# Four joins of a layer's output to x: last unit, root and first tiles by halves of the tokens

## The reference

```python
x = x + rms_norm(y, attn_post_g[layer])      # y = attention's output @ w_o
h = rms_norm(x, ffn_pre_g[layer])
f = swiglu(h, w_gate, w_up, w_down)
x = x + rms_norm(f, ffn_post_g[layer])       # then kv = rms_norm(x, kv_src_g) @ w_kv, or the next block
```

## Time and profile before

| | us |
|---|---|
| median of 3 runs | 1927.88 |
| the profiled execution | 1928.37 |
| its span | 1926.1 |
| TensorE busy, share of the span | 1908.9, 99% |
| VectorE | 954.8, 50% |
| ScalarE | 724.7, 38% |
| GpSimd | 738.0, 38% |

### The profile page before, as it was taken

The page is one execution under the profiler, slowest core; times in us unless marked ns, Lnnn a source line. Parts: engine busy times, 40 slices in busy tenths (PEclk is TensorE's granted clock), DMA queues, the critical chain, the costliest instruction groups (busy, mean ns, idle before and its releaser), DMA issues.

```text
span 1926.1 us, 22691 instructions
## 1 busy us (share of the span) xinstructions
PE 1908.9 (99%) x9056; PEld 1547.2 (80%) x9056; DVE 954.8 (50%) x1671; ACT 724.7 (38%) x1180; POOL 738.0 (38%) x313
## 2 busy tenths in 40 slices
PE   9999999999999999999999999999999999999998
PEld 7777888888888777888888888887777888888887
DVE  6662554442016545274444004796766755555203
ACT  6554422222234455342222224335654343333221
POOL 2333244444452322424444443343312444444442
PEclk9999999999999999999999999999999999999999
DMA  4512132223231222312222332321111223222232
GB/s 162 176 60 84 55 99 95 93 98 98 99 126 61 93 94 77 110 55 99 95 93 97 99 105 93 120 99 66 44 45 62 94 97 99 93 95 97 98 99 88
DMA packets 53305, 178.61 MB, mean 93 GB/s; under 512 B 5808, under 2 KB 8000, under 8 KB 52944
## 3 DMA queue, kind: packets, MB, share of 16 engines
q1 hardware_dynamic: 46928, 165.14, 26.1%
q10 hardware_dynamic: 6272, 12.02, 1.9%
HBM read 175.00 MB, written 6.33 MB: 94 GB/s over the span
## 4 chain that ended last, share of the span: by engine, by line
PE 96%; DVE 2%; ACT 1%; issue 1%; DMA 0%; SPq 0%; POOL 0%; DVEq 0%; ACTq 0%
PE bank L413 26%; PE bank L415 26%; PE bank L414 26%; PE bank L1563 2%; PE bank L1594 2%; PE bank L1548 1%; PE bank L1169 1%; PE bank L1163 1%; PE bank L1164 1%; PE bank L2024 1%; PE bank L1526 1%; PE bank L857 1%; PE bank L912 1%; PE bank L1046 1%; PE bank L1598 1%; PE bank L1040 1%
## 5 line engine op out<-in xcount | busy, mean ns | idle before, releaser
L393 POOL TENSOR_TENSOR wlo<-raw,whi 128x1024 fp32r<-128x1024 f32 x284 | 682.8, 2405 | 1140.1 <-ACT whi L388 1140.1
L388 ACT ACTIVATE whi<-raw 128x1024 fp32r<-128x1024 f32 x286 | 302.8, 1059 | 844.2 <-PE bank L415 813.0
L413 PE MATMUL bank<-hh,whi 128*128 128x512 f32 x1344 | 527.1, 392 | 1.2 <-DVE tmp L526 1.2
L415 PE MATMUL bank<-hh,wlo 128*128 128x512 f32 x1344 | 523.3, 389 | 0.0
L414 PE MATMUL bank<-hl,whi 128*128 128x512 f32 x1344 | 523.2, 389 | 0.0
L413 PEld LDWEIGHTS bank<-hh,whi 128*128 128x128 f32 x1344 | 252.3, 188 | 63.1 <-issue 9.8
L415 PEld LDWEIGHTS bank<-hh,wlo 128*128 128x128 f32 x1344 | 252.3, 188 | 52.6
L414 PEld LDWEIGHTS bank<-hl,whi 128*128 128x128 f32 x1344 | 252.4, 188 | 52.0 <-issue 0.5
L526 DVE TENSOR_TENSOR tmp<-bank,rs 128x512 f32<-128x512 f32 x154 | 105.3, 689 | 237.4 <-PE bank L415 223.5
L413 PE MATMUL bank<-fh,whi 128*128 128x512 f32 (+1 forms) x504 | 194.5, 386 | 0.0
L415 PE MATMUL bank<-fh,wlo 128*128 128x512 f32 (+1 forms) x504 | 194.5, 386 | 0.0
(11 more groups left out here) (304 smaller groups left out, 2475.3 us busy)
## 6 DMA issues: line engine op xcount, KB each, us to landing
raw<-stream SPq DMA_DIRECT2D x307, 512.0 KB, 3.4
bias_scratch<-rel_scratch ACTq DMA_DIRECT2D x1, 4096.0 KB, 18.1
biasB<-bias_scratch ACTq DMA_DIRECT2D x16, 256.0 KB, 2.8
w<-w_in ACTq DMA_DIRECT2D x2, 1024.0 KB, 5.8
x<-x_in SPq DMA_DIRECT2D x3, 512.0 KB, 9.3
out<-y SPq DMA_DIRECT2D x8, 128.0 KB, 1.9
out<-y ACTq DMA_DIRECT2D x8, 128.0 KB, 2.1
x<-x_in SPq DMA_DIRECT2D x2, 256.0 KB, 5.9
```

The source lines that it names most:

```text
L388: e.activation(slot[u][0][:, :], raw[u % 2][:, :], ACT.Copy).then_inc(*w_hi.done(u))
L393: e.tensor_tensor(slot[u][1][:, :], raw[u % 2][:, :], slot[u][0][:, :].bitcast(F32), ALU.subtract)\
L413: e.matmul(o, wh, h, start=first, stop=False)
L415: return e.matmul(o, wl, h, start=False, stop=last)
```

## The change

- The last unit of each of the four outputs is done by halves of the tokens: at oA and oB the last tile (`last_out_blocks_pe`), behind the down projections the last unit's four tiles (`last_down_pe`).
- Squares, sums, root, reciprocal and spread are made for each half by itself. Half 0's are interleaved with the products of half 1, and half 1's with the next layer's first products.
- The first tiles of the join (`AHEAD`: 2 at j0 and j2, 3 at j1 and j3) are done by halves, half 0 of all of them before half 1.
- `fill_clock` is no longer called at these four places.
- The copies of half 1 of the last four down tiles to y go from VectorE to ScalarE (`down_copy_act`).
- In the down projection's tail one unit is rounded, behind the root of half 0; the other is rounded in the join, behind the square of tile 1 (now in all four joins).
- Banks of the roots and of j1's and j3's squares are others.

```diff
-    def token_root_pe(e, key, spare, sums, ahead):
-        fill_clock(e, ahead, spare)
...
+    AHEAD = {"j0": 2, "j1": 3, "j2": 2, "j3": 3}
+    def root_sums_pe(e, key, half):
+        bk = bank[ROOT_AT[key][half]]
...
+        for t in tiles_of(half):
+            e.matmul(bk[:, t * P:(t + 1) * P], tmp[7][:, t * P:(t + 1) * P], ones, start=t == 2 * half, stop=False, skip_group_check=True)
+        e.wait_ge(*squared.at((key, KD - 1, half)))
+        for t in tiles_of(half):
+            mm = e.matmul(bk[:, t * P:(t + 1) * P], tmp[0][:, t * P:(t + 1) * P], ones, start=False, stop=t == 2 * half + 1, skip_group_check=True)
+        mm.then_inc(*summed.done((key, "tokens", half)))
...
     def out_pe(e, key, begun, ahead):
...
+        last_out_blocks_pe(e, u, 0, range(KD)).then_inc(*proj.done((key, KD - 1, 0)))
+        root_sums_pe(e, key, 0)
+        last_out_blocks_pe(e, u, 1, range(3))
+        root_spread_pe(e, key, 0)
+        last_out_blocks_pe(e, u, 1, range(3, KD)).then_inc(*proj.done((key, KD - 1, 1), ("unit", u)))
...
     def join_pe(e, key, outs, before):
...
+        half_high(0, 0)
+        root_sums_pe(e, before, 1)
+        half_low(0, 0)
+        half_high(1, 0)
+        e.wait_ge(*formed.at((key, "scaled", n - 1, 0)))
+        root_spread_pe(e, before, 1)
+        half_low(1, 0)
+        if n == 3:
+            half_high(2, 0)
+            half_low(2, 0)
+        half_high(0, 1)
+        for k in range(1, n):
+            half_high(k, 1)
+            half_low(k - 1, 1)
+        half_low(n - 1, 1)
+        for k in range(n, KD):
...
+    def join_act(e, key, before, gain, through, both=True):
+        n = AHEAD[key]
+        join_high_act(e, key, gain, 0, 0)
+        if before in ("oA", "oB"):
+            last_square_act(e, before, 1)
+        else:
+            down_last_act(e, before)
+        join_high_act(e, key, gain, 1, 0)
+        root_half_act(e, before, 1)
+        for k in range(2, n):
+            join_high_act(e, key, gain, k, 0)
+        for k in range(n):
+            join_high_act(e, key, gain, k, 1)
         for k in range(KD):
...
             square_tile(e, key, k, x[:, k, :], through)
-            if k == 1 and key in ("j0", "j2"):
+            if k == 1:
                 round_unit(e)
...
     def join_dve(e, key, before, post, gain, through, between=None):
+        e.wait_ge(*summed.at((before, "inverse", 0)))
+        join_half_tile(e, key, before, post, 0, 0)
+        if before not in ("oA", "oB"):
+            down_add_dve(e, before, 5, 1)
+            down_add_dve(e, before, 6, 1)
+        join_half_tile(e, key, before, post, 1, 0)
+        join_half_low(e, key, gain, 0, 0)
+        if before in ("oA", "oB"):
+            last_out_dve(e, before, 1)
+        join_half_low(e, key, gain, 1, 0)
+        root_half_dve(e, before, 1)
+        for k in range(2, n):
+            join_half_tile(e, key, before, post, k, 0)
+            join_half_low(e, key, gain, k, 0)
+        e.wait_ge(*summed.at((before, "inverse", 1)))
+        join_half_tile(e, key, before, post, 0, 1)
+        for k in range(1, n):
+            join_half_tile(e, key, before, post, k, 1)
+            join_half_low(e, key, gain, k - 1, 1)
+        join_half_low(e, key, gain, n - 1, 1)
+        for k in range(1, n - 1):
+            add_square(e, key, k, through)
+        join_tile(e, key, before, post, n)
...
+    def last_down_pe(e, key, u):
+        d = (key, "down")
+        for half, c in enumerate(HALVES):
+            for m in range(4, KD):
...
+                if half and m == 4:
+                    root_sums_pe(e, d, 0)
+                if half and m == 5:
+                    root_spread_pe(e, d, 0)
...
+    def down_tail_act(e, d):
+        e.wait_ge(*formed.at((d, "sq", 3)))
+        for m in range(4, KD):
+            down_square_act(e, d, m, 0)
+        down_square_act(e, d, 4, 1)
+        down_copy_act(e, d, 4)
+        root_half_act(e, d, 0)
+        round_unit(e)
+        for m in (5, 6):
+            down_square_act(e, d, m, 1)
+            if m == 5:
+                down_copy_act(e, d, m)
+
+    def down_last_act(e, d):
+        down_square_act(e, d, KD - 1, 1)
+        down_copy_act(e, d, 6)
+        down_copy_act(e, d, KD - 1)
```

More of the change, by code:

```diff
@@ new lines, in root_spread_pe, with root_half_act @@
+    def root_spread_pe(e, key, half):
+        e.wait_ge(*stats.at((key, "tokens", half)))
+        for t in tiles_of(half):
+            mm = e.matmul(bank[ROOT_AT[key][0]][:, t * P:(t + 1) * P], stat[:, 12 + t:13 + t].to_broadcast([P, P]), ident,
+                          start=True, stop=True)
+        mm.then_inc(*summed.done((key, "inverse", half)))
+    def root_half_act(e, key, half):
+        c = slice(2 * half, 2 * half + 2)
+        e.wait_ge(*summed.at((key, "tokens", half)))
+        e.activation(stat[:, 12 + 2 * half:14 + 2 * half], wide_sums(ROOT_AT[key][half])[:, c], ACT.Sqrt, scale=1.0 / D, bias=cc("eps"))\
+            .then_inc(*made.done((key, "root", half)))
@@ L1096, in token_root_dve, with last_out_blocks_pe @@
-    def token_root_dve(e, key):
-        e.wait_ge(*made.at((key, "root")))
-        e.reciprocal(stat[:, 12:16], stat[:, 12:16]).then_inc(*stats.done((key, "tokens")))
+    HALVES = (slice(0, T // 2), slice(T // 2, T))
+    LAST_BANK = (4, 5)
+    def last_out_blocks_pe(e, u, half, ks):
+        c = HALVES[half]
+        for k in ks:
+            mm = product(e, u, k, bank[LAST_BANK[half]][:, c], oh[:, k, c], ol[:, k, c], k == 0, k == KD - 1)
+        return mm
     def out_pe(e, key, begun, ahead):
@@ L1155, in of_high @@
             bk, out_key = outs[i]
             wh, wl = (w[:, k * P:(k + 1) * P] for w in slot[us[i]])
[L1157 to L1163, removed]
@@ L1222, in join_root_act, with join_tile @@
             round_unit(e)
[L1224 to L1233, removed]
+    def join_tile(e, key, before, post, k):
+        tb, r = 2 + k % 4, bank[ROOT_AT[before][0]]
+        e.tensor_tensor(tmp[tb][:, :], y[:, k, :], r[:, :], ALU.mult).then_inc(*formed.done((key, "scaled", k)))
         e.wait_ge(*formed.at((key, "scaled", k)))
@@ L1236, in join_tile, with join_half_tile @@
             .then_inc(*joined.done((key, k)))
-    def join_dve(e, key, before, post, gain, through, between=None):
-        e.wait_ge(*summed.at((before, "inverse")))
-        join_tile(e, key, post, 0)
-        for k in range(KD):
+    def join_half_tile(e, key, before, post, k, half):
+        tb, r, c = 2 + k % 4, bank[ROOT_AT[before][0]], HALVES[half]
+        e.tensor_tensor(tmp[tb][:, c], y[:, k, c], r[:, c], ALU.mult).then_inc(*formed.done((key, "scaled", k, half)))
+        e.wait_ge(*formed.at((key, "scaled", k, half)))
+        e.scalar_tensor_tensor(x[:, k, c], tmp[tb][:, c], gg(post, k), x[:, k, c], ALU.mult, ALU.add)\
+            .then_inc(*(joined.done((key, "half", k, 1), (key, k)) if half else joined.done((key, "half", k, 0))))
@@ L1283, in ffn_pe @@
                 end = kk == KF // 2 - 1 - (LAST_UNITS if conv and half else 0)
+                if end and half and not conv:
+                    last_down_pe(e, key, u)
+                    return
                 for r, m in ([(r, m) for m in range(4) for r in range(2)] if end
@@ L1601, in b_first_pe, with half_high, half_low @@
     def b_first_pe(e):
-        for k in range(KD):
-            if k % 2 == 0:
-                u = next_unit(e)
+        n, before = AHEAD["j1"], ("F0", "down")
+        us = [next_unit(e) for _ in range(2)]
+        def half_high(k, half):
+            e.wait_ge(*high.at(("j1", "half", k, half)))
+            for t in tiles_of(half):
+                if k == 0:
+                    join_free_pe(e, before, V_BANK[0][t])
+                values_high_pe(e, us[k // 2], 0, k, t)
+        def half_low(k, half):
+            e.wait_ge(*low.at(("j1", "half", k, half)))
+            for t in tiles_of(half):
+                mm = values_low_pe(e, us[k // 2], 0, k, t)
+            if k == 1 and half:
+                mm.then_inc(*proj.done(("unit", us[0])))
+        half_high(0, 0)
+        root_sums_pe(e, before, 1)
+        half_low(0, 0)
+        half_high(1, 0)
+        e.wait_ge(*formed.at(("j1", "scaled", n - 1, 0)))
+        root_spread_pe(e, before, 1)
+        half_low(1, 0)
+        half_high(2, 0)
+        half_low(2, 0)
+        half_high(0, 1)
+        for k in range(1, n):
+            half_high(k, 1)
+            half_low(k - 1, 1)
+        half_low(n - 1, 1)
+        for k in range(n, KD):
+            if k // 2 == len(us):
+                us.append(next_unit(e))
+            u = us[k // 2]
+            e.wait_ge(*high.at(("j1", k)))
             for t in range(QT):
-                if k:
-                    e.wait_ge(*high.at(("j1", k)))
-                else:
-                    e.wait_ge(*high.at(("j1", "half", t // 2)))
                 values_high_pe(e, u, 0, k, t)
```

243 lines of the change are left out of this document (143 added, 100 removed).

## The result

The changed kernel takes 1938.1 us (median of four runs, 1936.7 to 1940.5) against 1927.9: ratio 1.0054, 95% interval 1.0036 to 1.0071. It is 10.2 us slower; the forecast was 6.5 slower, 1934.4, with a range that ends at 1938.0. The sign and the waits came out as forecast. The size did not: there is one more cost on top of the waits, the clock, which the prediction had left out of its sum.

What follows compares the result with a forecast made beforehand. TensorE bounds the kernel, busy 1908.9 of 1926.1 us. Removed work of −12.6 us and added idle of +19.1 give +6.5 us, so 1934.4 against the median 1927.88; range 1925.5 to 1938.0.

Steps and rivals of the forecast that it cites:

- the waits: TensorE's idle at the four ends, walked through three in-order queues: 21.5 us against 2.4 before, +19.1.
- the clock: Rival (c), behind idle stretches at j1 and j3: 1.2 GHz for one tile each, +5.4, 1939.8 us; chance 0.10.
- The walk: Step-by-step timing of each of the four ends with prices read from the profile, counted from the last unit's first matmul.
- the walk's 12.10 and 16.76: Check on the kernel before: walked times of the join's first matmul (trace 12.28) and tile 3's late x (trace 16.85).
- The stops: VectorE's x and hl, with SBUF inputs, stand still while GpSimd's low part runs; six large ones of 1.71 to 1.86 us.
- Rival (a): GpSimd's part and x pass each other: 1925.6 us with no stop, 1928.6 or 1931.4 with one; chance 0.22.
- The bound that the prediction drew from the Trainium skill: Whichever of GpSimd and VectorE starts first keeps the shared ports, so a stop is at most a low part's 2.4 us.
- Work alone (rival b): At the four ends waits stay at 2.4 us and only the 12.6 us of removed work counts: 1915.3 us; chance 0.06.
- a clock under 1.00 beside the waits: Sign in the profile after that would show the forecast wrong: granted clock below 1.00 beside TensorE's waits near the joins.
- the argument "against": Against a falling clock: mean 0.89 after TensorE's last matmul, so the clock holds over a good part of an idle stretch.
- Fillers as waste: 66 of TensorE's 75 matmuls that compute nothing stand at the four ends and were counted as removable work.
- The 14.7 us: TensorE work gone at the four ends: 66 fillers at 0.2225 us each, −14.7 us, net −12.6 after added halves.

Runs made afterwards that it cites:

- three_fill: three_all with 69 matmuls that compute nothing in its gaps (14 before tile 3 at all joins, 9 and 4 before the first hh at j1 and j3): 1934.0 us.
- apart_both: The changed kernel with the down tail's rounding moved forward, the join's rounding moved back and square 1's add behind tile 3's low part: 1926.5 us, ratio 0.9992.
- low_split: The changed kernel with GpSimd's low part of the four units rounded at j1 and j3 cut into four quarter-width operations: 1931.5 us.
- three_all: The changed kernel with three tiles by halves at all four joins and the second half's reciprocal behind x of tile 2: 1944.2 us, two executions 1938.1 and 1938.6.
- no_fill: The kernel before the change without its 66 matmuls that compute nothing at the four ends: 1929.2 us, ratio 1.0006.
- best: apart_both with three tiles by halves at all joins, adds of squares 1 and 2 behind tile 3's hl, half 1's reciprocal behind x of tile 2: 1920.2 us.
- first_apart: The changed kernel with only the down tail's rounding moved forward, behind the half-0 square of tile 6: 1935.0 us.
- rr_h3: The changed kernel with the join's rounding moved behind the hh of tile 3 and square 1's add behind tile 3's hl: 1931.5 us.
- three_again: three_all run once more, unchanged, for one profile: 1942.7 us.
- three_split: three_all with adds of squares 1 and 2 behind tile 3's hl and GpSimd's low part of six units cut in four: 1924.9 us, ratio 0.9984.
- fill_waits: The changed kernel with nine and fourteen matmuls that compute nothing in the two long gaps at j1 and j3: 1935.7 us, ratio 1.0039.

## Why the prediction was right and where it failed

**The waits: right.** The walk gave 1934.4 for waits, work and stops; with the clock taken out by fillers, waits of this size measure 1934.0 (three_fill, walked within 0.1 of the change). Of the kernels walked with the same prices, the three that have no long gap, or a filled one, and whole low parts came out within 0.6 us (1926.5 for 1926.7, 1920.2 for 1920.8, 1934.0 for 1934.4). At j0 and j2 the change itself lies within 0.2 of its forecast. One reading was off without an effect on the forecast: the last unit at oA starts at 196.09, not 195.98, with 0.12 of waiting and not 0.23 before 202.54; the walk's 12.10 and 16.76 stand against 12.17 and 16.74.

**The stops: right.** 1.74 and 1.85 us for 1.7 and 1.86. Rival (a) is out. Moving the low parts off x gained 7.9 us (apart_both against 1934.4), and the walk gave 7.7. The bound that the prediction drew from the Trainium skill ("SBUF — State Buffer", "SBUF: two separate sides"), a stop of at most the GpSimd operation that x meets, held: 1.74 and 1.85 under 2.4, and in low_split 0.11 and 1.03 − 0.48 = 0.55 under a quarter's 0.7. What no row of before priced is how often x and hl meet one of several operations in a row.

**Work alone (rival b): out.** Idle in the four stretches is 16.6 us after, and was 0.3 before, when fillers stood in the waits.

**The failed step: the clock was a rival at 0.10 that excluded the forecast, when it was a term of the sum.** Its price was about right (5.4 given, 3.7 in the median, 6.6 at j1 and j3 of the profiled run). The prediction named a clock under 1.00 beside the waits as a sign of being wrong, and that sign is there. Its chance was wrong, and the argument "against" was the mistake: a mean of 0.89 in a window without a matmul was read as the clock holding over a gap. Between levels of 1 and a half that mean says that it fell 1.3 us before the window's end, after more than 4 us of idle. It does not show when it falls behind a gap in the middle: at the change's joins it fell behind 2.1, and three_all has the same gap with both outcomes. The walk itself had gaps of 2.1 and 3.9 us at two joins, of which the kernel before had none, since its fillers are there for that. With gaps walked, the clock belonged in the number: 1934.4 plus something between nothing and 5.4, so some 1937, and the range's upper end at 1940. The time was 0.1 above the end that I gave.

**Fillers as waste: half right.** Leaving them out gains nothing (no_fill), because they stand in waits. The 14.7 us were never a gain; only filling the waits with real work is, and best is the version that does that.

## What to carry to other kernels

When an edit takes real or dummy work off TensorE, walk the in-order queues to see which gaps appear, and price each gap like those here (2 to 3 us) twice: once as a wait, once as a half-rate stretch behind it that comes in some executions and not in others. An engine off the critical path (here GpSimd, 38% busy) can hold a two-input SBUF operation of VectorE for its whole length; place its work by the time at which it runs, not by where its queue has room, and give the engine that is stopped a lead of one tile.

## What the runs showed of the hardware

The clock fell at some gaps of TensorE and not at others of the same length. In the profiles of the change, first_apart, rr_h3, three_all and three_again, it fell in or behind 10 of the 12 gaps of 3.2 to 3.4 us at the joins (it held at j0 and j2 of three_all) and behind 3 of the 8 gaps of 2.1. It fell once behind 1.8 (first_apart at j2) and once behind 1.67 (no_fill at j2); the same 1.67 at the three other ends of no_fill left it at 1.00, as did 2.0 in low_split and three_split at j3. The windows from 10 to 20 us of low_split and apart_both have 0.83 as well, with no gap over 1.3 us before them; the change has 1.00 there. So the length of one gap does not decide it.

At j1 of the change the window behind the gap of 2.1 has 0.83, which is 3.4 us at the lower level, and behind the one of 3.4 the pace was half for 5.7 us, although TensorE had no gap in them. Four to fourteen matmuls of 128 columns in the gaps of fill_waits and three_fill kept the clock at 1.00 in every window profiled at the joins.

A GpSimd subtraction of 1024 columns takes 2.4 us when an x of VectorE is issued behind it, and x ends 0.3 to 0.6 after it; it took 2.67 where VectorE's hl was already running when it began. Cut in four it takes 3.0 to 3.7: the quarters take 0.7 each, and 0.9 or 1.2 where they find an x or hl under way.
